# Whole f32 values in place of a high and a low part in two TensorE stages of a mixture-of-experts block, and two shared steps in other places

## What is computed

```python
scores = jax.nn.sigmoid(jnp.dot(t, w_router))
sel = scores + router_bias                      # groups of 8, the best 4 groups, the best 8 experts
...
out = (jax.nn.silu(t @ ws_gate) * (t @ ws_up)) @ ws_down
for e in range(N_EXPERTS):
    hid = jax.nn.silu(t @ we_gate[e]) * (t @ we_up[e])
    out = out + gates[:, e:e + 1] * (hid @ we_down[e])
```

## Time and profile before

| | |
|---|---|
| median of three runs | 695.98 us |
| the profiled execution | 690.9 us, span 689.1 us |
| TensorE busy | 623.2 us (90% of the span) |
| TensorE weight loads | 346.7 us (50%, beside the products) |
| DVE, ACT, GpSimd busy | 256.1, 125.9, 44.4 us |
| bytes read from HBM | 248.9 MB, 363 GB/s over the span |
| mean granted TensorE clock | 0.972 of full |

### The profile page before, as it was taken

The page is one execution under the profiler, slowest core; times in us unless marked ns, Lnnn a source line. Parts: engine busy times, 40 slices in busy tenths (PEclk is TensorE's granted clock), DMA queues, the critical chain, the costliest instruction groups (busy, mean ns, idle before and its releaser), DMA issues.

```text
span 689.1 us, 11735 instructions
## 1 busy us (share of the span) xinstructions
PE 623.2 (90%) x4454; PEld 346.7 (50%) x4454; DVE 256.1 (37%) x704; ACT 125.9 (18%) x269; POOL 44.4 (6%) x225
## 2 busy tenths in 40 slices
PE   2599999999789999999899999979899999999792
PEld 0278877744445454454344445544445445544440
DVE  0129938869562233241323232331133132332115
ACT  2311312202510111211111111110111111111113
POOL 7000000000400000101000000010000001000000
PEclk9789999999998999999999999999999999999996
DMA  8996894565378999999999999999999999999951
GB/s 346 380 400 267 334 394 160 214 272 212 156 290 360 411 418 422 420 420 419 420 421 420 421 420 421 419 421 419 422 419 422 419 421 419 421 420 421 420 208 63
DMA packets 39868, 250.75 MB, mean 364 GB/s; under 512 B 4657, under 2 KB 6785, under 8 KB 11777
## 3 DMA queue, kind: packets, MB, share of 16 engines
q1 hardware_dynamic: 38256, 248.56, 88.1%
q10 hardware_dynamic: 1554, 1.41, 0.6%
HBM read 248.91 MB, written 1.05 MB: 363 GB/s over the span
## 4 chain that ended last, share of the span: by engine, by line
PE 70%; DMA 15%; DVE 9%; ACT 3%; issue 1%; SPq 1%; ACTq 0%; DVEq 0%
PE PS L1371 11%; PE PS L1581 10%; PE PS L1577 10%; DMA ring<-in_we_up_dram 9%; PE PS L1556 8%; PE PS L1618 5%; PE PS L1587 5%; PE PS L1613 4%; DMA ring<-in_w_in_dram 4%; PE PS L1640 3%; PE PS L1636 2%; PE PS L1623 2%; DVE MOD L885 2%; PE PS L1501 1%; PE PS L1596 1%
## 5 line engine op out<-in xcount | busy, mean ns | idle before, releaser
L1371 PE MATMUL PS<-hT,ring 128*128 128x256 f32 x384 | 86.8, 386 | 3.7 <-DMA ring<-in_w_in_dram 3.7
L1581 PE MATMUL PS<-ring,arena 128*64 128x256 f32 x736 | 88.4, 391 | 0.3 <-DMA ring<-in_we_up_dram 0.3
L1192 DVE SCALAR_TENSOR_TENSOR arena<-arena,gate,PS 128x128 f32<-128x128 f32 (+1 forms) x44 | 16.6, 378 | 175.8 <-ACT arena L809 175.8
L1371 PEld LDWEIGHTS PS<-hT,ring 128*128 128x128 f32 x384 | 73.8, 194 | 15.1 <-issue 5.2
L1203 DVE TENSOR_TENSOR YLO<-PS,YHI 128x512 fp32r<-128x512 f32 x54 | 37.2, 689 | 97.0 <-ACT YHI L820 97.0
L1556 PE MATMUL PS<-G,H2HI 128*128 128x256 f32 (+1 forms) x240 | 63.6, 300 | 10.4 <-ACT arena L800 7.0
L1577 PE MATMUL PS<-ring,arena 128*32 128x512 f32 x576 | 68.6, 628 | 3.8 <-DMA ring<-in_we_up_dram 3.8
L1581 PEld LDWEIGHTS PS<-ring,arena 128*64 128x64 f32 x736 | 50.3, 134 | 32.5 <-issue 4.0
L820 ACT CAST YHI<-PS 128x512 fp32r<-128x512 f32 x54 | 31.6, 586 | 161.4 <-PE PS L1618 79.2
L1556 PE MATMUL PS<-G,H2LO 128*128 128x256 f32 (+1 forms) x240 | 59.1, 281 | 0.0
L1556 PEld LDWEIGHTS PS<-G,H2HI 128*128 128x128 f32 x240 | 46.1, 192 | 22.7 <-issue 9.6
(11 more groups left out here) (265 smaller groups left out, 606.2 us busy)
## 6 DMA issues: line engine op xcount, KB each, us to landing
ring<-in_we_gate_dram SPq DMA_DIRECT2D x64, 1024.0 KB, 16.4
ring<-in_we_up_dram SPq DMA_DIRECT2D x64, 1024.0 KB, 19.2
ring<-in_we_down_dram SPq DMA_DIRECT2D x64, 1024.0 KB, 16.6
ring<-in_w_ada_dram SPq DMA_DIRECT2D x6, 3072.0 KB, 15.1
ring<-in_w_in_dram SPq DMA_DIRECT2D x3, 3072.0 KB, 15.9
ring<-in_w_ada_dram SPq DMA_DIRECT2D x3, 2048.0 KB, 7.1
ring<-in_w_out_dram SPq DMA_DIRECT2D x1, 3072.0 KB, 19.4
ring<-in_w_in_dram SPq DMA_DIRECT2D x1, 1568.0 KB, 26.8
```

Source lines behind the costliest of these rows:

```text
L1371: mm = pe.matmul(PS[:, 2 + q % QB, 0:TOK], w[:, k, (m % 6) * P:(m % 6) * P + P], hT[:, k, :], start=(k == 0), stop=(k == KD - 1))
L1581: m = pe.matmul(PS[64 * c:64 * c + 64, 6, 0:FE].rearrange("p (a n) -> p a n", a=2), xt[:, k, :], gu_cols(w[0], k, c), start=(k == 0), stop ...
```

## The change

Four things. G, SCAT and the y rows become plain f32 (Y in place of YHI and YLO). H2HI and H2LO are gone with `high_part` and GpSimd's subtraction; the gather reads H2P itself, each block of features as every eighth column. Each product of the gather and of add_up is made once. `y_low` is gone, and what waited for it waits for the copy `y_copy` (ACT). `scatter_matrix` of position p waits for add_up of position p - 2. H2P has another place in memory. And in the two places where two shared gate-up products stood ahead of the logits of tile 1 and ahead of the sort's product, one stands now, and the other behind.

```diff
-        H2HI = nc.alloc_sbuf_tensor_at("H2HI", [P, TT, D], F32R, offset=h2_at)
-        H2LO = nc.alloc_sbuf_tensor_at("H2LO", [P, TT, D], F32R, offset=h2_at + 4 * TT * D)
-        YHI = nc.alloc_sbuf_tensor_at("YHI", [P, D], F32R, offset=y_at)
-        YLO = nc.alloc_sbuf_tensor_at("YLO", [P, D], F32R, offset=y_at + 4 * D)
-        G = nc.alloc_sbuf_tensor_at("G", [P, 2, TT, 256], F32R, offset=gffn_at)
+        Y = nc.alloc_sbuf_tensor_at("Y", [P, D], F32, offset=y_at)
+        G = nc.alloc_sbuf_tensor_at("G", [P, 2, TT, 256], F32, offset=gffn_at)
...
-                pool.tensor_tensor(H2LO[:, t, :].rearrange("p (k q) -> p k q", k=KD),
-                                   H2P[:, t, :].rearrange("p (q k) -> p k q", k=KD),
-                                   H2HI[:, t, :].rearrange("p (k q) -> p k q", k=KD).bitcast(F32),
-                                   ALU.subtract).then_inc(h2lo_ready, 1)
...
-                if t == 0:
-                    high_part(0)
...
-            high_part(1)
...
-            def y_high(p, h):
+            def y_copy(p, h):
                 act.wait_ge(down_ps, parts_before(p) + h + 1)
-                act.copy(y_part(YHI, p, h), bank(5)).then_inc(yhi_ready, 1)
+                act.copy(y_part(Y, p, h), bank(5)).then_inc(y_ready, 1)
...
             def scatter_matrix(p):
+                if p >= 2:
+                    dve.wait_ge(summed, p - 1)
                 dve.tensor_scalar(SCAT[:, p % 2, :], tokrow, tokf[:, p:p + 1], None,
                                   ALU.is_equal).then_inc(scat_ready, 1)
...
-                for h in range(halves(p)):
-                    y_low(p, h)
...
                         for t in range(TT):
-                            for part_no, h2 in enumerate((H2HI, H2LO)):
-                                m = pe.matmul(PS[:, xt_bank(n), 256 * half:256 * half + w], h2[:, t, k * P:(k + 1) * P],
-                                              G[:, i % 2, t, 0:w], start=(t == 0 and part_no == 0),
-                                              stop=(t == TT - 1 and part_no == 1))
+                            m = pe.matmul(PS[:, xt_bank(n), 256 * half:256 * half + w], H2P[:, t, k:D:KD],
+                                          G[:, i % 2, t, 0:w], start=(t == 0), stop=(t == TT - 1))
...
-                pe.wait_ge(ylo_ready, parts_before(p) + half)
+                pe.wait_ge(y_ready, parts_before(p) + half)
...
-            shared_gate_up(0, range(1, 3))
+            shared_gate_up(0, range(1, 2))
             logits(1)
-            shared_gate_up(0, range(3, KD))
+            shared_gate_up(0, range(2, KD))
             shared_gate_up(1, range(0, 1))
...
-            shared_gate_up(1, range(1, 3))
+            shared_gate_up(1, range(1, 2))
```

More of the change, by code:

```diff
@@ L367, in build @@
         down_ps = sem("down_ps")
-        yhi_ready = sem("yhi_ready")
-        ylo_ready = sem("ylo_ready")
+        y_ready = sem("y_ready")
         scat_ready = sem("scat_ready")
@@ L754, in _ @@
             copy_mod_rows(range(6))
-            def high_part(t):
-                act.copy(H2HI[:, t, :].rearrange("p (k q) -> p k q", k=KD),
-                         H2P[:, t, :].rearrange("p (q k) -> p k q", k=KD)).then_inc(h2hi_ready, 1)
             def shared_silu(t):
@@ L831, in _ @@
                     copy_xT(UNIT_OF[p] + 1, pairs)
-                y_high(p, 0)
+                y_copy(p, 0)
                 if p + 1 < NPOS:
@@ L835, in _ @@
                 if halves(p) == 2:
-                    y_high(p, 1)
+                    y_copy(p, 1)
             over = act.value_load(oflag[0:1, 0:1], min_val=0, max_val=1)
@@ L850, in _ @@
                             act.wait_ge(more_down_ps, e * 2 + (2 * NE * r + half + 1))
-                            act.copy(YHI[:, 512 * half:512 * half + 512], bank(5)).then_inc(more_yhi, 1)
+                            act.copy(Y[:, 512 * half:512 * half + 512], bank(5)).then_inc(more_y, 1)
             with act.Else():
@@ L1279, in _ @@
                                                  op1=ALU.mult).then_inc(more_hid, 1)
[L1280 to L1284, removed]
                         dve.wait_ge(more_done, e + (NE * r + 2))
@@ L1628, in add_up @@
             def add_up(p):
-                pe.wait_ge(ylo_ready, parts_before(p + 1))
+                pe.wait_ge(y_ready, parts_before(p + 1))
                 pe.wait_ge(scat_ready, p + 1)
                 for t in range(TT):
[L1633 to L1642, removed]
+                    for c in range(2):
+                        if halves(p) == 2:
+                            m = pe.matmul(bank(2 * t + c), SCAT[:, p % 2, t * P:(t + 1) * P], y_part(Y, p, c),
+                                          start=False, stop=True, skip_group_check=True)
+                        else:
+                            m = pe.matmul(bank(2 * t + c), SCAT[64 * c:64 * c + 64, p % 2, t * P:(t + 1) * P],
+                                          Y[64 * c:64 * c + 64, 0:512], start=False, stop=True,
+                                          skip_group_check=True)
                 m.then_inc(summed, 1)
@@ L1671, in _ @@
                       stop=True).then_inc(order_ps, 1)
-            shared_gate_up(1, range(3, KD))
+            shared_gate_up(1, range(2, KD))
             shared_hidden_transposes(0)
@@ L1732, in _ @@
                                 for t in range(TT):
[L1733 to L1736, removed]
+                                    m = pe.matmul(PS[:, 4, place * P:(place + 1) * P], H2P[:, t, k:D:KD],
+                                                  G[:, 0, t, 0:P], start=(t == 0), stop=(t == TT - 1))
                             m.then_inc(more_xT_ps, 1)
@@ L1756, in _ @@
                             m.then_inc(more_down_ps, 1)
-                        pe.wait_ge(more_ylo, e * 2 + (2 * NE * r + 2))
+                        pe.wait_ge(more_y, e * 2 + (2 * NE * r + 2))
                         pe.wait_ge(more_scat, e + (NE * r + 1))
                         for t in range(TT):
-                            for y in (YHI, YLO):
-                                for c in range(2):
-                                    m = pe.matmul(bank(2 * t + c), SCAT[:, 0, t * P:(t + 1) * P],
-                                                  y[:, 512 * c:512 * c + 512], start=False, stop=True,
-                                                  skip_group_check=True)
+                            for c in range(2):
+                                m = pe.matmul(bank(2 * t + c), SCAT[:, 0, t * P:(t + 1) * P],
+                                              Y[:, 512 * c:512 * c + 512], start=False, stop=True,
+                                              skip_group_check=True)
                         m.then_inc(more_done, 1)
```

24 lines of the change are left out of this document (5 added, 19 removed).

## The result

The changed kernel takes 772.53 us (772.08 to 772.90, four runs) against 695.85 us before: a ratio of 1.1103, 95% interval 1.1084 to 1.1123. The sign and the new limit were forecast (slower, TensorE in place of the transfers), the size was not: 753 with a range up to 768. The profiled execution took 772.17 us (span 770.4), 81.3 more than the profiled one before, which lay 5 us under its own median.

The account below looks back on a forecast made before the run. Transfers were taken as the limit, with TensorE only 8.8 us from being one too. Terms summed to +58.8 us, on the median 696.0 giving 754.8, taken as 753 us; own range 746 to 760, wider range 744 to 768.

Parts of the forecast that it names:

- What bounds: Routed experts' stage: transfers have no room, TensorE only 8.8 us of waits; work added beyond that moves the end.
- Two rows a product, each up to twice as long: Gather and adding-up: half the products, two f32 rows each, so as many rows; 0.434 us replaces 0.236 at 256 columns.
- I charge nothing for the step.: Gather: weights read 8 values apart cost nothing extra, as strided transposes step by 0.11 us, under 0.164.
- the term of the gather: Gather without unit 0: 3.17 us more per 256-column unit, 1.66 per 192-column unit, +35.3 us in all.
- strided loads become the limit: Rival, gather: loads at twice 0.11 us raise 192-column rows from 0.164 to 0.22, 10.8 us more, 764 us; chance 0.05.
- Row tiles in f32: Rival, adding-up with one half: row tiles overlap partly, 768 us (chance 0.08), or not at all, 806 us (0.04).
- Waits and half clock: Experts' stage: TensorE's waits for weights vanish, -8.8 us, and two half-clock dips behind them, -2.6 us.
- The low part of y: DVE's step at L1203 goes; half of TensorE's 2.6 us of waits for it counted: -1.3 us.
- The head: Before position 0's gate-up: logits start at 177.3 instead of 180.52, first sorted load 4.2 us earlier; -5.2 us in all.
- three pairs fill the whole stretch: Unit 0's gather: its first three pairs take 5.2 us and fill TensorE's 2.62 us wait for DVE.
- The 5.1 us added at the end: Median of the runs lies 5.1 us above the profiled 690.9, so the sum was put on 696.0: 754.8, not 749.7.

Follow-up runs that it names:

- the light kernel: Kernel before with all products of the low parts left out, the low parts still made and waited for: 690.68 us, ratio 0.9946.
- The execution of 695.46 us above: Traced execution of the kernel before with only two shared gate-up products moved, behind the logits and the sort's product; that run measured 693.14 us, ratio 0.9994.
- the freed head: Kernel before with the shared products moved as in the change and h2's high parts made in ACT's gaps: 689.23 us, ratio 0.9948.

## Why the prediction was wrong

1. **What bounds.** Right. TensorE had 8.8 us of waits to fill, they are gone, and the light kernel shows the transfers at the other side of it.
2. **Two rows a product, each up to twice as long.** Right: 480 rows for 240 products, no rows saved.
3. **"I charge nothing for the step."** This is the step that failed. I took the rate at which strided transposes follow each other, 0.11 us, for the rate of any strided load. A transpose's load is a shorter one, though: it took 140 ns side by side and 193 strided, where the f32 product's took 190 and 336. Why a transpose loads faster no run shows. Strided f32 loads step by 0.24 us, above the 0.217 and 0.164 of the products, so the load sets the gather's pace, and units of 192 columns cost as much as those of 256. That is 24.5 us by the run with weights side by side, and it takes the forecast from 753 to 777; measured 772.5. Without it the kernel takes 748.0, within my range and 5 us under the forecast, and the gather of units 1 to 14 costs 100.19 - 65.21 = +35.0 us, where my term was +35.3. So the term of the gather was wrong by its loads alone.
4. **The rival was named and priced too low.** I had "strided loads become the limit" at twice 0.11, 0.22, worth 11 us and 0.05 of the chance. The basis was again the transposes' rate. With 0.24, the step above 0.217 counts in the wide units as well.
5. **Row tiles in f32** run side by side: 1.92 us, 0.05 more than the column tiles of the earlier trace rows. That rival falls.
6. **Waits and half clock.** Right in size, and gone as said. The clock was at full from 40 us to the end of TensorE's work. The low part of y brought 3.2 us and not 1.3: besides the 2.6 us that I halved I had left out the wait of 1.7 us at L1613.
7. **The head.** Right to about half a microsecond up to the gather (177.64, 185.84), then 1.6 us short. About 1 us of it is the dear loads of unit 0's gather: in the run with weights 1 value apart, whose logits start 0.2 us later, gate-up 0 ends at 211.03 in place of 211.87. The rest is a step that failed by itself. I had three pairs fill the whole stretch in which TensorE waited 2.62 us for DVE, but 0.96 us of that wait stays, in that run too.
8. **The 5.1 us added at the end.** I had worked the sum out from a trace of 690.9 us and then put it on the median of 696.0. Executions of the kernel before take from 690.1 to 697.8 us. Those above 695 have a mean clock of 0.963 to 0.968, those below 691 one of 0.970 to 0.975. The four of the changed kernel lie within 0.9 us. The execution of 695.46 us above has 5 us at half clock in the routing, and its first sorted load goes out at 196.49 and not at 193.35. The changed kernel has neither the wait for h2 ahead of that stretch nor the half clock. So I read the 5.1 us as time of a kind that the change takes away, which should not have been added: 749.7 + 24.5 = 774.2, against 772.17 in the trace. That all long executions are of this kind is not shown, and the routing is not the only place: the freed head, without that wait, still takes from 686.7 to 691.5.

## What to carry to other kernels

Ask of each matmul which is longer, its stream or its weight load, and take the load's price from rows with the same type, mode and stride. Weights that are every eighth value in memory were cheap in a transpose here and dear in a product; a store of DVE that puts them side by side, at 2.00 us a tile in place of 1.28, was worth 24.5 us. Where two limits stand within 9 us of each other in 450, work added to either costs nearly its full price and work removed gains next to nothing: first count the waits on the other one. And when a sum made from one trace is put on a median, look whether the difference between the two is time that the change removes.

## What was not expected of the hardware

- Weight loads of 128 columns, 4-byte values: 190 ns at 4 bytes apart, 197 at 8, 329 at 16, 336 at 32. At 16 and 32 they follow each other at 0.24 us. That is for f32; for fp32r, 192 at 4 bytes apart and 337 at 32.
- f32 products in two row tiles of 64 rows run side by side: eight rows of 512 columns in 1.92 us, where eight full ones, one after the other, take 3.44.
- Beside GpSimd's subtraction (2.9 us) DVE's steps grew from 1.28 to 2.25 us, from 0.29 to 1.46, and a `tensor_scalar` of 16 columns from 0.18 to 2.07, which has one SBUF tensor alone as its input.
